# Two chained transformer blocks on one core: all weight blocks of the modulation loaded ahead of the first expert gather and summed as a table of rows, and two weight loads of the second block issued at another expert

## The reference, cut to what matters

```python
def expert_block(args):
    hc, ec, gc = args
    uc = jnp.take(u, ec, axis=0)
    a = jnp.einsum('cd,ced->ce', hc, uc)
    act = jax.nn.gelu(a, approximate=False) * gc
    vc = jnp.take(v, ec, axis=0)
    return jnp.einsum('ce,ced->cd', act, vc)
```

## Time and profile before

| | us |
|---|---|
| median of 3 runs | 2395.04 (2388.01 to 2404.72) |
| profiled execution, its own time | 2395.91 |
| its span, first to last instruction | 2394.1 |
| TensorE busy | 2124.7 |
| VectorE busy | 1231.1 |
| ScalarE busy | 825.3 |
| GpSimd busy | 593.8 |

### The profile page before, as it was taken

The page is one execution under the profiler, slowest core; times in us unless marked ns, Lnnn a source line. Parts: engine busy times, 40 slices in busy tenths (PEclk is TensorE's granted clock), DMA queues, the critical chain, the costliest instruction groups (busy, mean ns, idle before and its releaser), DMA issues.

```text
span 2394.1 us, 24307 instructions
## 1 busy us (share of the span) xinstructions
PE 2124.7 (89%) x8264; PEld 1254.5 (52%) x8264; DVE 1231.1 (51%) x2915; ACT 825.3 (34%) x2356; POOL 593.8 (25%) x548
## 2 busy tenths in 40 slices
PE   6879998888989787999888888879999999999998
PEld 4545554434545333555433343427756667766665
DVE  2356867755767675686776667743620002441001
ACT  1244544433554344354444344532410001331000
POOL 1123435333334343243544344420000000000000
PEclk9889999999999999999999999999999999989999
DMA  9969999999999999899999999992434432343420
GB/s 391 418 265 426 427 427 427 427 426 427 426 427 412 426 427 406 359 423 427 427 427 427 427 426 427 427 421 90 157 151 162 155 130 75 115 173 118 164 109 18
DMA packets 107712, 767.01 MB, mean 320 GB/s; under 512 B 12210, under 2 KB 12482, under 8 KB 15939
## 3 DMA queue, kind: packets, MB, share of 16 engines
q0 software_dynamic: 78336, 570.46, 56.8%
q1 hardware_dynamic: 29252, 195.00, 20.6%
HBM read 764.36 MB, written 1.05 MB: 320 GB/s over the span
## 4 chain that ended last, share of the span: by engine, by line
PE 57%; DMA 26%; DVE 9%; ACT 5%; issue 2%; POOL 1%; DVEq 0%; SPq 0%; ACTq 0%; POOLq 0%
PE PS L517 55%; DMA BIG<-in_uv,EID 21%; DMA MOD<-in_uv,EID 4%; DVE BIG L1597 3%; DMA BIG<-in_win 1%; ACT DG L950 1%; POOL BIG L460 1%; ACT L1139 1%; PE PS L577 1%; DVE BIG L1303 1%; PE PS L610 1%; DVE SC L1366 1%; ACT AV L950 1%; DVE H L1303 0%; ACT BIG L1025 0%
## 5 line engine op out<-in xcount | busy, mean ns | idle before, releaser
L517 PE MATMUL PS<-BIG,DG 128*128 128x512 f32 x1820 | 892.2, 627 | 170.5 <-ACT DG L950 158.4
L1597 DVE CUSTOM_DVE_ANT_0 BIG<-BIG,H 128x1024 f32<-128x1024 f32 x455 | 558.6, 1228 | 331.8 <-DMA BIG<-in_uv,EID 300.1
L460 POOL DMA_INDIRECT BIG<-in_uv,EID x455 | 510.8, 1123 | 815.4 <-PE PS L517 762.8
L517 PEld LDWEIGHTS PS<-BIG,DG 128*128 128x128 f32 x1820 | 335.2, 197 | 623.4 <-ACT DG L950 305.0
L517 PE MATMUL PS<-HT,BIG 128*128 128x128 f32 (+1 forms) x2304 | 383.2, 323 | 8.4 <-DMA BIG<-in_wq 4.1
L517 PEld LDWEIGHTS PS<-HT,BIG 128*128 128x128 f32 x2304 | 349.5, 192 | 75.7 <-issue 45.4
L1139 ACT ACTIVATE AV<-AV 128x1 f32<-128x1 f32 x512 | 103.1, 201 | 646.7 <-DVE AV L1597 642.6
L517 PE MATMUL PS<-BIG,HT 128*128 128x256 f32 (+3 forms) x1216 | 301.4, 406 | 21.4 <-DMA BIG<-in_win 10.8
L517 PE MATMUL PS<-BIG 128*128 128x512 f32 (+7 forms) x792 | 280.9, 525 | 1.7 <-DVE BIG L1289 1.7
L517 PEld LDWEIGHTS PS<-BIG,HT 128*128 128x128 f32 x1216 | 231.9, 197 | 92.5 <-issue 48.5
L1293 DVE TENSOR_TENSOR BIG<-BIG 128x256 f32<-128x256 f32 (+1 forms) x96 | 49.3, 514 | 383.5 <-ACT BIG L1274 381.3
(11 more groups left out here) (168 smaller groups left out, 1274.2 us busy)
## 6 DMA issues: line engine op xcount, KB each, us to landing
BIG<-in_win SPq DMA_DIRECT2D x36, 1024.0 KB, 4.9
BIG<-in_wup SPq DMA_DIRECT2D x32, 1024.0 KB, 6.9
BIG<-in_wdn SPq DMA_DIRECT2D x32, 1024.0 KB, 4.8
BIG<-in_wada POOLq DMA_DIRECT2D x29, 1024.0 KB
BIG<-in_wq SPq DMA_DIRECT2D x28, 1024.0 KB
BIG<-in_wout SPq DMA_DIRECT2D x24, 1024.0 KB, 5.6
BIG<-in_wada SPq DMA_DIRECT2D x16, 1024.0 KB
BIG<-in_uv,EID POOLq DMA_INDIRECT x455
```

Of the source, the lines that this page charges most:

```text
L460: pool.e.indirect_dma_start(out=slot(u), out_offset=None, in_=I[f"uv{l}"], in_offset=bass.IndirectOffsetOnAxis(ap=EID[:, t * 128 + j:t * 1 ...
L517: return pe.e.matmul(dst, a, b, start=start, stop=stop)
L1597: v.e.tensor_tensor_reduce(out=JD, in0=slot(u)[:, 0:1024], in1=H[:, t, :], scale=1.0, scalar=0.0, op0=ALU.mult, op1=ALU.add, accum_out=AV[ ...
```

## The change

All 48 blocks are loaded by GpSimd ahead of the gathers. Those of layer 1 (24) are multiplied by `row`: the condition stands in one column of a cleared tile (`ZC`), and its window of 32 columns is shifted so that block b's sum lands in row b of each row group; all 24 add up in one PSUM bank. At step 6 of pass 0 VectorE adds the biases, which came with one load into rows 8 to 23 of the tile `ROWS`, and stores the table there. Two small matmuls with a selection matrix turn rows 0 to 7 into the columns of the first norm. For each of the 16 later blocks, VectorE masks the table to the rows of that block (a scaling by a 0/1 column) at its step of `LATE`, TensorE spreads it as before and ScalarE copies it as before. The first twelve of these steps are 90 to 112 instead of 106 to 128. The bias rows and the 16 loads are gone from SyncE's queue. B0 and B1 are loaded after the dot product of expert 126 instead of 122.

```diff
-EARLY = 32
-LATE = [106 + 2 * i for i in range(12)] + [2 * 129 + 10 + 2 * i for i in range(4)]
+LATE = [90 + 2 * i for i in range(12)] + [2 * 129 + 10 + 2 * i for i in range(4)]
...
-LAST = [GSLOTS[(EARLY + 512 + i) % len(GSLOTS)] for i in range(len(GSLOTS))]
+LAST = [GSLOTS[(len(ADA) + 512 + i) % len(GSLOTS)] for i in range(len(GSLOTS))]
...
-            def late():
-                k = Clock()
-                for i, (l, b) in enumerate(ADA[EARLY:]):
-                    yield from k.to(LATE[i])
-                    load(in_w, ("ada", l, b), I["wada"][l * 24 + b], 2048, ("pe.ada", l, b))
-                    if b > 8:
-                        sp.wait_ge(*at("v.part", 1, b - 1))
-                    sp.e.dma_start(BIAS[0:1, :], I["bada"][1:2, b * 256:(b + 1) * 256]).then_inc(*landed("ld_bias", b))
...
+            sp.e.dma_start(ROWS[8:24, :], I["bada"][1:2, 2048:6144].rearrange("a (b n) -> (a b) n", n=256)).then_inc(*landed("ld_rows"))
...
-                sp.wait_ge(*at("v.dot", 3, 122))
+                sp.wait_ge(*at("v.dot", 3, 126))
...
-            for l, b in ADA[0:EARLY]:
+            for l, b in ADA:
...
-                if 8 <= k < 18:
-                    next(early)
+                if k >= 8:
+                    next(early, None)
+            for _ in early:
+                pass
...
+            def row(l, b):
+
+                key = ("ada", l, b)
+                u = in_g.where[key]
+                w = slot(u).rearrange("p (k n) -> p k n", k=8)
+                if b == 0:
+                    pe.wait_ge(*at("v.zc"))
+                    pe.wait_ge(*at("v.bias", "m", 0, 0, 1))
+                pe.wait_ge(*at(f"ga{u}", *key))
+                for k in range(8):
+                    j = k % 4 * 32
+                    p = mm(PS[j:j + 32, 2, 0:256], ZC[:, k, 31 - b:63 - b], w[:, k, :], b == 0 and k < 4, b == 23 and k >= 4)
+                p.then_inc(*up("pe.ada", l, b))
...
             def late():
                 k = Clock()
-                todo = ADA[EARLY:]
-                for i, x in enumerate(todo):
+                yield from k.to(WHEN["rows"] + 2)
+                pe.wait_ge(*at("v.rows"))
+                for c in range(2):
+                    p = mm(PS[:, 2, 256 + c * 8:264 + c * 8], ROWS[:, c * 128:(c + 1) * 128], CST[:, C_SEL:C_SEL + 8], True, True)
+                p.then_inc(*up("pe.adc"))
+                for i, x in enumerate(ADA[32:]):
                     yield from k.to(LATE[i] + 1)
                     if x in BATCH:
                         pe.wait_ge(*at("v.bias", "m", *BATCH[x], 1))
-                    matvec(*x, in_w, in_b)
...
+                    spread(*x, in_b)
...
             def late():
                 k = Clock()
-                for i, x in enumerate(ADA[EARLY:]):
-                    yield from k.to(LATE[i] + 2)
-                    partial(*x, in_b)
+                yield from k.to(WHEN["rows"])
+                v.wait_ge(*at("pe.ada", 1, 23))
+                v.wait_ge(*at("ld_rows"))
+                tt(ROWS, PS[:, 2, 0:256], ROWS, ALU.add).then_inc(*up("v.rows"))
...
+                for i, (l, b) in enumerate(ADA[32:]):
+                    yield from k.to(LATE[i])
+                    v.wait_ge(*at("pe.adb", *((l, b - 2) if b > 9 else (0, b + 14))))
+                    ts(ACC[:, b % 2, 0:256], ROWS, CST[:, C_SEL + b:C_SEL + b + 1], None, ALU.mult, None).then_inc(*up("v.part", l, b))
...
+            v.e.memset(ZC, 0.0).then_inc(*up("v.c"))
+            cp(ZC[:, :, 31:32], COND[:, 16:24].unsqueeze(2)).then_inc(*up("v.zc"))
```

More of the change, by code:

```diff
@@ L23 @@
 EPS = 1e-6
-C_ID, C_ND, C_ROPE, C_IOTA, C_END = 0, 128, 640, 1024, 1040
+C_ID, C_ND, C_ROPE, C_IOTA, C_SEL, C_END = 0, 128, 640, 1024, 1040, 1064
 C_SM = C_ND
@@ L401, in hold_map @@
                 hold(in_2, ("s", l, g), ("pe.pv", "s", l, g))
-            drive(pre, head, nothing(), late(), lambda p, b: None, lambda p: None, enter)
+            drive(pre, head, nothing(), nothing(), lambda p, b: None, lambda p: None, enter)
             for l in range(L):
@@ L465, in nothing @@
         def nothing():
-            while True:
-                yield True
+            yield True
         def drive(pre, head, early, late, experts, finish, enter):
@@ L517, in mm, with matvec @@
                 return pe.e.matmul(dst, a, b, start=start, stop=stop)
-            def matvec(l, b, ring, banks):
+            def matvec(l, b, banks):
                 key = ("ada", l, b)
-                u = ring.where[key]
+                u = in_g.where[key]
                 w = slot(u).rearrange("p (k n) -> p k n", k=8)
@@ L545, in early @@
             def early():
-                for blocks in (ADA[0:8], ADA[8:20], ADA[20:EARLY]):
+                for blocks in (ADA[0:8], ADA[8:20], ADA[20:24]):
                     for i, x in enumerate(blocks):
-                        matvec(*x, in_g, in_a)
+                        matvec(*x, in_a)
                         if i > 0:
@@ L553, in early @@
                     yield True
+                for x in ADA[24:]:
+                    row(*x)
+                    yield True
             def late():
                 k = Clock()
-                todo = ADA[EARLY:]
-                for i, x in enumerate(todo):
+                yield from k.to(WHEN["rows"] + 2)
[4 more added lines that the diff above has]
+                for i, x in enumerate(ADA[32:]):
                     yield from k.to(LATE[i] + 1)
@@ L561, in late @@
                         pe.wait_ge(*at("v.bias", "m", *BATCH[x], 1))
-                    matvec(*x, in_w, in_b)
[L563 to L567, removed]
+                    _, freed = in_b.take(("ada", *x), ("a.ada", *x))
+                    if freed:
+                        pe.wait_ge(*at(*freed))
+                    spread(*x, in_b)
             def transposes(l, t, which, h):
@@ L978, in late @@
                 k = Clock()
-                todo = ADA[EARLY:]
-                for i, x in enumerate(todo):
+                for i, x in enumerate(ADA[32:]):
                     yield from k.to(LATE[i] + 2)
-                    partial(*x, in_b)
[L983 to L987, removed]
+                    modulation(*x, in_b)
             def rms_in_hT(name, key, t, srcs, D):
@@ L1328, in modulation, with whole_gain @@
                     if b == 7:
-                        g, n = MC[:, l * 16 + 8:l * 16 + 16], NC[:, l * 8:l * 8 + 8]
-                        stt(g, g, 1.0, n, ALU.add, ALU.mult).then_inc(*up("v.cols", l))
+                        whole_gain(l)
+            def whole_gain(l):
+                g, n = MC[:, l * 16 + 8:l * 16 + 16], NC[:, l * 8:l * 8 + 8]
+                stt(g, g, 1.0, n, ALU.add, ALU.mult).then_inc(*up("v.cols", l))
             def early():
-                for blocks in (ADA[0:8], ADA[8:20], ADA[20:EARLY]):
+                for blocks in (ADA[0:8], ADA[8:20], ADA[20:24]):
                     for i, x in enumerate(blocks):
```

28 lines of the change are left out of this document (18 added, 10 removed).

## The result

| | median (runs) | ratio to before, 95% interval |
|---|---|---|
| before | 2394.96 us (8) | |
| changed kernel | 2385.24 us (2380.8 to 2388.73; 8) | 0.9956 [0.994, 0.9973] |

What follows compares the result with a forecast made beforehand. Up to about 1610 us time was bytes over 427 GB/s plus stretches without DMA work, then TensorE's. From 2395.9 us, -18 + 1.5 - 8 - 7.3 = -31.8 gave 2364.1, as a median 2363; range 2352 to 2380.

Steps and rivals of the forecast that it cites:

- Step 1: Sixteen weight blocks moved ahead of the first gather fill missing transfer at 120 to 160 us: 18 us gained, bounds 10 to 22.6.
- The two gaps: Transfer still missing among the moved blocks: 1.6 us before 130 us and 2.2 us around 133, 3.8 in all.
- the boundary of passes 0 and 1: Without the late blocks the DMA engines may lack supply where these passes meet: 1.5 us charged, 0 to 3.
- the test that the prediction gave: A first dot near 177 but pass 0 not ending about 18 us earlier would refute the moved blocks' gain.
- Step 2: In pass 2 SyncE no longer waits for VectorE, so w_in loads go out earlier: 8 us gained, bounds 3 to 12.6.
- The dry window: DMA engines run dry at 960 to 970 us in pass 2 after a late w_in load: 6.3 us missing, expected to go.
- Rival A: TensorE paces pass 2's beginning, so freeing SyncE gives 2 us, not 8: 2369 us; chance 0.14.
- Step 3: At pass 3's end, block two's first loads wait for expert 126, so the last gathers come 2.46 us apart: 7.3 us gained.
- the landing: Block two's first load lands 4.9 us after its issue, just ahead of the projection that reads it.
- B: The passes keep TensorE's pace, not DMA's: -3 us, 2392, or half-way 2378; chance 0.11 with the half-way case.
- C: Pass 0 begins at half clock and stays there, so the kernel is slower: +11 us, 2406; chance 0.04.
- D: The ring holds the added loads until after the expert numbers, so moving blocks gives zero: 2381 us; chance 0.05.

Runs made afterwards that it cites:

- the aligned kernel: The changed kernel with scratch tile SC 24 columns smaller, so BIG starts at byte 110336 as in the kernel before: 2363.06 us, ratio 0.9873.

## Why the prediction was wrong

**The step that failed** is the premise of the sum, that "up to about 1610 us the time is bytes divided by 427 GB/s". Its bytes were right; the rate was read off the kernel before and taken for a constant of the chip, when it depends on where BIG starts. The line of the diff that widens CST stood in plain sight and was costed at nothing, and not even named. It cost 20 to 23 us of a gain of 32. None of the rivals named it: all four took terms of the schedule. Without it the forecast of 2363 stands beside a measured 2363.06. That closeness is luck, as the parts miss in both directions:

- **Step 1, right.** GpSimd's wait is gone; the first dot is at 178.3, or 178.0 with BIG in place, predicted 176.9. Of 22.7 us missing 20.5 are filled; predicted were 18.8 of 22.6. The two gaps cost 2.2 us in all, where 3.8 were expected from the rows. The prediction's estimate from the Trainium skill, DMA: Bandwidth & Descriptors, on the anatomy of one DMA, had them half a microsecond shorter each, 2.8; the measured sum is nearer to that, though not gap by gap: some 0.4 is missing before 132 us and 1.6 from 132 to 136. At the boundary of passes 0 and 1, 0.7 more is missing (from 180 to 900 us) where 1.5 was charged. But the test that the prediction gave, pass 0 ending some 18 us earlier, was wrong twice. Its 18 counts all sixteen blocks, of which four leave pass 2 and not pass 0: by its own numbers, a start 21.5 later and 12 x 2.46 = 29.5 given back, pass 0 should end 8 earlier. It ends 3.8 later. The twelve blocks no longer hold SyncE back, so it fetches weights of the next pass while pass 0 runs. SyncE with BIG in place, then before:

```profile
399.36 0.43 SPq L323 DMA_DIRECT2D BIG<-in_win  x1
...
488.41 0.80 SPq L323 DMA_DIRECT2D BIG<-in_win  x2
```

```profile
533.78 4.09 SPq L323 DMA_DIRECT2D BIG<-in_win  x3
```

  Three such loads are 7.4 us. By the end of pass 0 227.06 MB have been moved, for 217.35 before: the time isn't lost, it has been spent on later passes. The four blocks of pass 2 and those three loads are 7.3 of the 9.7 MB; the rest wasn't traced back. The gain then shows at the ends of passes 1 and 2 (-8.8, -22.8).
- **Step 2, oversized.** Predicted 8 us, bounds 3 to 12.6. The dry window goes as described, but of 11.1 us that are filled in the changed kernel 5.9 come back behind 1060 us, about half of it where passes 2 and 3 meet. By the medians it is worth 1 to 4 us, neither told from zero; from first dot to last 4.1 and 2.2 us, one pair of executions each. Rival A, that TensorE paces this stretch, had the size (2 us) and not the reason: the transfers do run, and later ones go missing. Why just there wasn't tried.
- **Step 3, right.** 7.3 predicted, 7.0 measured on top of the others; alone 4.3 by the medians, 7.1 from first dot to last. The loads go out at 1587.73 in the aligned kernel, the projection starts 5.3 us later at 1593.07 without a wait: 4.9 us for the landing fit in with 0.4 to spare.
- **Rivals B, C, D.** From the first dot to the end of pass 3 are 1415.3 us with BIG in place, for 1467.2: 51.9 less, where TensorE's pace would have allowed 12.8 + 4.3 + 7.3 = 24.4 (B). The granted clock: 0.50 from 180 to 185 us and 0.87 in the next 5 in the changed kernel, for 0.50 and 0.79 in the first two such windows before, so the passes do not begin at half clock for longer than before (C):

```profile
180.00:185.00 5.00, 4.27 (x8) 2.24 (x9) 4.05 (x11) 3.43 (x8) 0.25 (x1) 0.50 1.02 426
185.00:190.00 5.00, 5.00 (x21) 3.38 (x21) 4.54 (x17) 3.69 (x10) 1.49 (x2) 0.87 1.02 426
```

The added loads start at 127.69 us, while the expert numbers were there only shortly before 149.87 in the kernel before: the ring doesn't hold them (D).

What stays open: the worth of the freed SyncE, some 2 to 4 us, more closely; why the missing transfer turns up at the meeting of passes 2 and 3; and what in the chip makes the difference between starts.

## What to carry to other kernels

When a kernel is paced by DMA, its rate is a term of the sum like any other: compare the plateau of GB/s and the DMA share first, before any wait; a lower plateau at the same share is a slower transfer, not a new stall. Before costing an edit, list which tiles grow or shrink and what is laid out behind them, and keep tiles that take large DMA rows on multiples of 256 bytes (a smaller scratch tile did it here, for 20 us). A stretch of missing transfer that is filled counts in full only if the same transfer isn't lost again later; sum what is missing over the whole span. And when a whole kernel scatters by more than the edit is worth, measure in the trace between two events that enclose the edit's stretch: here that told 2 and 4 us where the medians told nothing.

## What the runs showed of the hardware

The start of a tile in SBUF sets what an 8192-byte packet into it costs: 309.0 ns on a multiple of 256 bytes, 313.2 on the mean at 96 past one (without the 1% above 330); 427 or 421 GB/s. The loss does not grow with the distance: 421 GB/s at 64, 96 and 128 bytes, 422 with the ninth slot well placed. The Trainium skill, DMA: Bandwidth & Descriptors, How a descriptor splits into AXI transactions, has a descriptor cut into pieces of 256 bytes, where one that starts elsewhere begins with a piece from the boundary below, whose unused bytes still cost. Worked out from it, an estimate: 8192 bytes take 256 beats on a boundary and 258, 259 or 260 at 64, 96 or 128 past it, 0.8, 1.2 or 1.6% more. The runs agree in sign and order, 1.3 to 1.4% by packets and 1.4% by rate, but not in the grading: the mean packet takes 313.3, 313.2 and 313.1 ns. The section speaks of what is fetched; here it is the start of the destination that was moved.

One more thing wasn't expected. The slot in MOD stood 128 bytes past a multiple in the kernel before, and yet 98.8% of all packets there took 309 ns, its own, one gather in nine, among them. A single badly placed slot among well placed ones showed no cost; eight of nine did, and there the one well placed slot made its own packets and the next slot's fast. So a packet's time seems to hang on its neighbours too. No run was made to say why.
